# First four weight tiles sliced by chunk and multiplied beside the input's chunks, on one Trainium2 core

## The chip, the core and the metric

The kernel runs on one core of a Trainium2 chip. The metric is the device time of one execution in microseconds. Three runs of the kernel before gave 1047.52, 1047.68 and 1048.74 us, median 1047.68. Engines are named as the profile names them: PE is TensorE's matmul, PEld its weight load, DVE is VectorE, ACT is ScalarE, POOL is GpSimd, SP is SyncE, which issues the DMAs.

## The reference, cut to what matters

The reference is two transformer blocks of width 1024 on 512 tokens, in float32. What the change touches is the very beginning of the first block, the norm and the first part of its input projection:

```
h = x * rsqrt(mean(x * x) + 1e-6) * norm_mix_pre
proj = h @ w_in                      # 1024 -> 5120 columns
conv_in, q, k, v, g_conv, g_att = split(proj)
u = conv_in[:, :512] * sigmoid(conv_in[:, 512:])     # GLU, 8 tiles of 128 columns
u = causal depthwise convolution of 31 taps over u   # and so on
```

Attention, convolution branch, merge, feed-forward and the second block follow and stay as they are.

## The kernel before, in words

Activations lie transposed: 128 partitions are 128 features, 512 columns are the tokens, and the 1024 features are 8 chunks (KC). The weights come from HBM as a stream of 160 units. One unit is what one output tile of 128 features needs from all 8 chunks, 128x1024 floats, 512 KB. It lands in one of four slots of w_raw.

To keep float32 accuracy with the fast matmul, each operand is split in two parts: a high part (a_hi, w_hi), rounded by ACT with a Copy, and a low part (a_lo, w_lo), the rest, which DVE makes for the activations and POOL for most weights by a subtraction of two SBUF operands. A product of one chunk is three matmuls into the same bank: hi by hi (L442), activations' low by weights' high (L443), weights' low (L444). So a unit is 24 matmuls of 128x512.

The norm is applied late. The matmuls use x times the gain alone; the factor of each token, 1/rms, is multiplied in when DVE drains a bank (`drain`, L1624) with scale_row. For scale_row ACT squares the 8 chunks (sq_x, L1082), DVE adds them in place in seven steps (`add_square`, L1601), PE sums over partitions (`total`, L476, which waits for acc_ready and takes bank 6), DVE and ACT make the root (`norm`, `std`), PE turns it into a row (`spread`, L509, bank 7), and ACT copies the row (`row`, L1061). No tile can be drained before that.

Each engine works through an order written out by hand, with semaphores between engines. The beginning, before the change:

- SP (L404 to L414) issues the gain, then the eight chunks of x (256 KB each) with the two halves of unit 0 among them, then units 1, 2 and 3, then the other vectors. After that `load` (L416) refills a slot of w_raw when lo_ready says that its last unit has been split.
- ACT (L1067 to L1087) makes a_hi of each chunk as it lands, w_hi of unit 0's halves after chunks 0 and 2, then unit 1's, then the squares with unit 2's w_hi after two of them, then units 3, 4 and 5 as slots come free.
- DVE (L1613 to L1621) makes a_lo of each chunk (`low_scaled`, L1565), three half low parts of units 0 and 1 (`half_low`), then the seven adds, then the norm.
- POOL makes constants (L2191 to L2217), then the last half of unit 1's low part (L2225), then units' low parts in order (`ahead`, `low_weights`, L2185), of units 2 to 5 in the first round of its loop.
- PE (L529 to L556) waits for all 14 constants, then computes unit 0 chunk by chunk as chunks come, then units 1 and 2, `total`, unit 3 with `spread` in its middle, then units 4 to 7, of which 4 and 5 reuse banks 0 and 1 and wait for their drain, then the token tiles of v (L516).

After its norm DVE drains tiles 0 to 3, with a GLU product after each pair, and then works on the convolution's taps (`some_taps`, L1631, which accumulates in banks 4 and 5) with the drains of later tiles between them (L1742 to L1763).

Of the kernel before, what the change touches and what calls it, by code (L numbers as in the profile page):

```python
# [7 lines left out]
F32 = mybir.dt.float32  # L8
# [6 lines left out]
P = 128  # L15
# [63 lines left out]
def two_layer_block(nc, xT, vecs, wstream, outT):  # L79
    with ExitStack() as ctx:  # L80
# [12 lines left out]
        def sem(name):  # L93
            return ctx.enter_context(nc.semaphore(name))
# [160 lines left out]
        half_loaded, half_hi, half_lo = sem("half_loaded"), sem("half_hi"), sem("half_lo")  # L255
# [143 lines left out]
        @block.sync  # L399
        def _(sp_eng):  # L400
            def load_x(c):
                sp_eng.dma_start(resid[:, c, :], xT[:, c, :]).then_inc(x_loaded[c], 16)

            sp_eng.dma_start(vec[:, 0:KC], vecs[:, 0:KC]).then_inc(gain_loaded, 16)  # L404
            load_x(0)
            sp_eng.dma_start(w_raw[:, 0, 0:UNIT // 2], wstream[0][:, 0:UNIT // 2]).then_inc(half_loaded, 16)
            load_x(1)
            load_x(2)
            sp_eng.dma_start(w_raw[:, 0, UNIT // 2:], wstream[0][:, UNIT // 2:]).then_inc(raw_loaded[0], 16)
# [25 lines left out]
            sp_eng.wait_ge(stored, 16 * KC)  # L435
# [3 lines left out]
        def _(pe):  # L439
# [76 lines left out]
            def token_tiles(u0):  # L516

                for u in range(4):
# [7 lines left out]
                                          w_hi[:, u % 2, w], w_lo[:, u % 2, w], first=c == 0, last=c == KC - 1)  # L526
                    mm.then_inc(units_done, 1)

            pe.wait_ge(consts, CONSTS)  # L529


            for c in range(KC):
                pe.wait_ge(split_lo, c + 1)
                if c % 4 == 0:
                    pe.wait_ge(half_lo, c // 4 + 1)
                w = slice(c * P, (c + 1) * P)
                mm = products(ps[:, 0, :], w_hi[:, 0, w], w_lo[:, 0, w], a_hi[:, c, :], a_lo[:, c, :],
                              first=c == 0, last=c == KC - 1)
            mm.then_inc(units_done, 1)
            for c in range(KC):  # L540
                if c == 0:
                    pe.wait_ge(half_lo, 3)
                if c == KC // 2:
                    pe.wait_ge(lo_ready, 2)
                w = slice(c * P, (c + 1) * P)
                mm = products(ps[:, 1, :], w_hi[:, 1, w], w_lo[:, 1, w], a_hi[:, c, :], a_lo[:, c, :],
                              first=c == 0, last=c == KC - 1)
            mm.then_inc(units_done, 1)
            unit_tile(2, 0, 2, a_hi, a_lo)
            total(sq_x, 1)  # L550
            unit_tile(3, 1, 3, a_hi, a_lo, middle=lambda: spread(r_exp0, 0))
            for n in range(4, 8):
                pe.wait_ge(tile_drained, CREDIT + (n - 3 if n < 6 else 1))
# [478 lines left out]
        def _(act):  # L1032
# [34 lines left out]
            for c in range(KC):  # L1067
                act.wait_ge(x_loaded[c], 16)
                act.activation(a_hi[:, c, :], resid[:, c, :], ACT.Copy, scale=col("g_mix_pre", c)).then_inc(split_hi, 1)
                if c == 0:  # L1070
                    act.wait_ge(half_loaded, 16)
                    act.activation(w_hi[:, 0, 0:UNIT // 2], w_raw[:, 0, 0:UNIT // 2], ACT.Copy).then_inc(half_hi, 1)
                if c == 2:
                    act.wait_ge(raw_loaded[0], 16)
                    act.activation(w_hi[:, 0, UNIT // 2:], w_raw[:, 0, UNIT // 2:], ACT.Copy).then_inc(half_hi, 1)
            act.wait_ge(raw_loaded[1], 16)
            act.activation(w_hi[:, 1, 0:UNIT // 2], w_raw[:, 1, 0:UNIT // 2], ACT.Copy).then_inc(half_hi, 1)
            act.activation(w_hi[:, 1, UNIT // 2:], w_raw[:, 1, UNIT // 2:], ACT.Copy).then_inc(hi_ready, 1)
            for c in range(KC):
                if c == 2:  # L1080
# [468 lines left out]
        def _(dve):  # L1549
# [57 lines left out]
            def half_low(n):  # L1607
                k, at_half = n // 2, n % 2
                w = slice(at_half * UNIT // 2, (at_half + 1) * UNIT // 2)
                dve.wait_ge(half_hi, n + 1)  # L1610
                low(w_lo[:, k, w], w_raw[:, k, w], w_hi[:, k, w]).then_inc(half_lo, 1)
# [134 lines left out]
            for n, (a, b) in ((4, (0, 6)), (5, (6, 12)), (None, (12, 14)), (6, (14, 19)), (7, (19, 25)), (None, (25, 27))):  # L1746
# [435 lines left out]
        def _(pool):  # L2182
# [26 lines left out]
            for h in range(8):  # L2209
# [241 lines left out]
def _stream(w_in, w_conv_branch, w_att_branch, w_out, w_up, w_down, w_in_2, w_out_2):  # L2451
# [67 lines left out]
```

## Time and profile before

| | us |
|---|---|
| median of three runs | 1047.68 |
| the profiled execution's own time | 1047.43 |
| its span, first to last instruction | 1045.7 |
| PE busy in the span | 1025.2 |
| DVE busy | 522.4 |
| ACT busy | 458.4 |
| POOL busy | 519.2 |

The span is what the profiler saw between the first and the last instruction of the program; 1.7 us of the execution's own time lie outside it. A row of the timeline has the start in us from the span's begin, the time taken, the engine, the line, the operation with output and inputs, the shapes, a count of instructions merged into the row, and in brackets how long the engine sat idle before it and what ended that. The durations of matmuls overlap, because they are pipelined; from one start to the next is what a matmul costs.

### The profile page before, as it was taken

The numbers are of one execution on the slowest core, as the hardware profiler recorded it, in microseconds if no ns is written. First come the engines' busy times: TensorE is split into PE (matmuls) and PEld (weight loads), VectorE is DVE, ScalarE is ACT, GpSimd is POOL, SyncE is SP. The second block draws the span as 40 slices with busy tenths as digits, with TensorE's granted clock in tenths as the row PEclk, the third lists the DMA queues.
The fourth block names the chain that finished last, engine by engine and source line by source line (L and its number), as shares of the span: only waits on it lengthen the run. The fifth ranks groups of instructions, "written<-read, shape, count | busy, mean of one in ns | idle before, by whom it ended". The sixth has DMA issues, their size and how long they took to land.

```text
span 1045.7 us, 13313 instructions
## 1 busy us (share of the span) xinstructions
PE 1025.2 (98%) x4898; PEld 844.2 (81%) x4898; DVE 522.4 (50%) x839; ACT 458.4 (44%) x667; POOL 519.2 (50%) x300
## 2 busy tenths in 40 slices
PE   7999999999999999999999999999999999999998
PEld 5888888788888787888888888887888777777787
DVE  6899785554362555434434311003624176685731
ACT  5322345888752433223332222223354357476540
POOL 3444565933534423444444446445286554665562
PEclk9999999999999999999999999999999999999999
DMA  6233221111142313222232233324122211111112
GB/s 236 94 101 100 83 85 57 61 61 61 61 181 83 118 41 101 94 87 100 100 100 94 88 112 108 101 100 141 41 80 81 81 61 42 61 60 42 41 61 81
DMA packets 25965, 91.03 MB, mean 87 GB/s; under 512 B 3008, under 2 KB 3136, under 8 KB 25792
## 3 DMA queue, kind: packets, MB, share of 16 engines
q1 hardware_dynamic: 25920, 90.42, 25.7%
q8 instruction: 30, 0.49, 0.2%
q14 instruction: 15, 0.12, 0.0%
HBM read 88.31 MB, written 2.10 MB: 86 GB/s over the span
## 4 chain that ended last, share of the span: by engine, by line
PE 86%; DVE 5%; POOL 3%; issue 3%; ACT 2%; DMA 0%; SPq 0%; POOLq 0%; DVEq 0%; ACTq 0%
PE ps L442 26%; PE ps L444 26%; PE ps L443 26%; POOL w_lo L2185 2%; DVE s L2026 1%; PE ps L839 1%; PE ps L863 1%; PE ps L588 1%; POOL sp_lo L2237 1%; PE ps L582 1%; PE ps L484 1%; PE ps L568 1%; PE ps L471 0%; ACT s L1409 0%; DVE pt_lo L1562 0%
## 5 line engine op out<-in xcount | busy, mean ns | idle before, releaser
L2185 POOL TENSOR_TENSOR w_lo<-w_raw,w_hi 128x1024 fp32r<-128x1024 f32 x146 | 347.6, 2381 | 422.5 <-ACT w_hi L1040 373.1
L1040 ACT ACTIVATE w_hi<-w_raw 128x1024 fp32r<-128x1024 f32 (+1 forms) x140 | 146.3, 1045 | 287.4 <-PE ps L444 287.3
L442 PE MATMUL ps<-a_hi,w_hi 128*128 128x512 f32 x560 | 224.3, 400 | 9.9 <-DVE w_lo L1562 7.2
L444 PE MATMUL ps<-a_hi,w_lo 128*128 128x512 f32 x560 | 219.1, 391 | 0.0
L443 PE MATMUL ps<-a_lo,w_hi 128*128 128x512 f32 x560 | 219.0, 391 | 0.0
L442 PE MATMUL ps<-b_hi,w_hi 128*128 128x512 f32 x408 | 159.4, 391 | 1.0 <-POOL w_lo L2185 0.8
L444 PE MATMUL ps<-b_hi,w_lo 128*128 128x512 f32 x408 | 158.8, 389 | 0.0
L443 PE MATMUL ps<-b_lo,w_hi 128*128 128x512 f32 x408 | 158.7, 389 | 0.0
L442 PEld LDWEIGHTS ps<-a_hi,w_hi 128*128 128x128 f32 x560 | 105.6, 189 | 36.1 <-issue 9.1
L444 PEld LDWEIGHTS ps<-a_hi,w_lo 128*128 128x128 f32 x560 | 105.6, 189 | 22.8
L443 PEld LDWEIGHTS ps<-a_lo,w_hi 128*128 128x128 f32 x560 | 105.9, 189 | 21.1 <-issue 0.5
L442 PEld LDWEIGHTS ps<-b_hi,w_hi 128*128 128x128 f32 x408 | 76.6, 188 | 17.4 <-POOL w_lo L2185 1.2
L444 PEld LDWEIGHTS ps<-b_hi,w_lo 128*128 128x128 f32 x408 | 76.6, 188 | 16.0
L443 PEld LDWEIGHTS ps<-b_lo,w_hi 128*128 128x128 f32 x408 | 76.6, 188 | 15.8
L1645 DVE SCALAR_TENSOR_TENSOR ps<-u_pad,vec,ps 128x512 f32<-128x512 f32 x112 | 75.5, 748 | 0.0
L443 PE MATMUL ps<-h_lo,w_hi 128*128 128x512 f32 x176 | 68.5, 389 | 0.0
L444 PE MATMUL ps<-h_hi,w_lo 128*128 128x512 f32 x176 | 68.5, 389 | 0.0
L442 PE MATMUL ps<-h_hi,w_hi 128*128 128x512 f32 x176 | 68.5, 389 | 0.0
L1558 DVE TENSOR_TENSOR up_h<-up_u,up_s 128x512 f32<-128x512 f32 x22 | 49.4, 2246 | 21.5 <-ACT up_s L1302 21.3
L1558 DVE TENSOR_TENSOR up_u<-ps,scale_row 128x512 f32<-128x512 f32 x22 | 15.2, 690 | 83.4 <-PE ps L444 83.4
L1558 DVE TENSOR_TENSOR sq_f<-sq_f 128x512 f32<-128x512 f32 x13 | 9.8, 752 | 82.5 <-ACT sq_f L1326 81.9
L1409 ACT ACTIVATE s<-s,smax 128x384 f32<-128x384 f32 (+2 forms) x64 | 35.2, 552 | 16.8 <-DVE smax L2009 16.8
(324 smaller groups left out, 1591.8 us busy)
## 6 DMA issues: line engine op xcount, KB each, us to landing
w_raw<-weights SPq DMA_DIRECT2D x159, 512.0 KB, 3.2
resid<-x_t SPq DMA_DIRECT2D x8, 256.0 KB, 5.3
resid<-x_t SPq DMA_DIRECT2D x1, 2048.0 KB, 8.0
out_t<-out_sb SPq DMA_DIRECT2D x8, 256.0 KB, 2.0
w_raw<-weights SPq DMA_DIRECT2D x2, 256.0 KB, 4.5
vec<-vecs SPq DMA_DIRECT2D x1, 220.0 KB, 8.3
vec<-vecs SPq DMA_DIRECT2D x1, 4.0 KB, 1.8
```

The costliest lines, as they stand in the source:

```text
L442: pe.matmul(out, s_hi, m_hi, start=first, stop=False, skip_group_check=True)
L443: pe.matmul(out, s_hi, m_lo, start=False, stop=False, skip_group_check=True)
L444: return pe.matmul(out, s_lo, m_hi, start=False, stop=last, skip_group_check=True)
L484: pe.matmul(ps[:, 5, :], tri[:, :], src, start=True, stop=True, skip_group_check=True)
L568: pe.matmul(z_of(h)[:, o:o + (TB - j) * P], k[r, key], q[r, j * P:T], start=j != 3 and t == 0, stop=False, skip_group_check=True)
L582: pe.matmul(z[:, w], tri[:, :], parts[:, w], start=False, stop=False, skip_group_check=True)
L588: mm = pe.matmul(z[:, o:o + width], neg_ones[:, :], parts[:, Z_COL[j2]:Z_COL[j2] + width], start=False, stop=False, skip_group_check=True)
L1040: act.activation(w_hi[:, k % 2, 0:width], w_raw[:, k, 0:width], ACT.Copy).then_inc(hi_ready, 1)
L1409: e = act.activation(s2[:, head, w], s2[:, head, w], ACT.Exp, scale=-1.0, bias=smax[:, head, b:b + 1], accum_out=den[:, kind_of(c), half_o ...
L1558: return dve.tensor_tensor(out, in0, in1, op)
L1645: V.do(dve.scalar_tensor_tensor(out=acc if k == TAPS - 1 else part, in0=src, scalar=w, in1=part, op0=ALU.mult, op1=ALU.add))
L2185: pool.tensor_tensor(w_lo[:, k % 2, 0:width], w_raw[:, k, 0:width], w_hi[:, k % 2, 0:width].bitcast(F32), ALU.subtract).then_inc(lo_ready, 1)
```

## The change

The first four units are no longer stored tile by tile but chunk by chunk. The host packs units 0 to 3 so that one slice, 128x512, holds the weights of one chunk for all four tiles. Slices are loaded alternately with the chunks of x. PE multiplies chunk by chunk into four banks. Their high and low parts lie in buffers of their own (wf_hi, wf_lo, in the place of b_hi and b_lo), so units 4 and 5 find both slots of w_hi and w_lo free. POOL makes six of the eight low slices, DVE the first two. The sum of the squares (`total`) stands before the last chunk's matmuls, `spread` after them. Tile 4 gets bank 4 and no wait, and DVE drains it before the taps begin. ACT makes the high parts of units 4 and 5 right after the squares. Sixteen matmuls on a constant (WARM) stand ahead of everything on PE.

```
+WARM = 16
+        wf_hi = place("wf_hi", [P, KC, UNIT // 2], F32R, at["b_hi"])
+        wf_lo = place("wf_lo", [P, KC, UNIT // 2], F32R, at["b_lo"])
+        def slices(c):
+            return w_raw[:, c // 2, c % 2 * (UNIT // 2):(c % 2 + 1) * (UNIT // 2)]
-        GLU_BANKS, QK_BANKS, LO_BANKS = (0, 1, 2, 3, 0, 1, 6, 7), (6, 7), (0, 6, 7, 6)
+        GLU_BANKS, QK_BANKS, LO_BANKS = (0, 1, 2, 3, 4, 1, 6, 7), (6, 7), (0, 6, 7, 6)
 # SP
-            load_x(0)
-            sp_eng.dma_start(w_raw[:, 0, 0:UNIT // 2], ...).then_inc(half_loaded, 16)
-            load_x(1)
-            load_x(2)
-            sp_eng.dma_start(w_raw[:, 0, UNIT // 2:], ...).then_inc(raw_loaded[0], 16)
-            for c in range(3, KC):
+            for c in range(KC):
                 load_x(c)
-            for k in range(1, 4):
-                sp_eng.dma_start(w_raw[:, k, :], wstream[k]).then_inc(raw_loaded[k], 16)
+                load_slices(c)
             sp_eng.dma_start(vec[:, KC:], vecs[:, KC:]).then_inc(vec_loaded, 16)
...
-            sp_eng.wait_ge(half_lo, 3)
 # PE
+            pe.wait_ge(consts, 6)
+            for _ in range(WARM):
+                pe.matmul(ps[:, 5, 0:P], neg_ones[:, :], neg_ones[:, :], start=True, stop=True, ...)
             pe.wait_ge(consts, CONSTS)
             for c in range(KC):
+                if c == KC - 1:
+                    total(sq_x, 1)
+                pe.wait_ge(split_hi, c + 1)
+                pe.wait_ge(slice_hi, c + 1)
+                for k in range(4):
+                    pe.matmul(ps[:, k, :], wf_hi[:, c, k * P:(k + 1) * P], a_hi[:, c, :], ...)
                 pe.wait_ge(split_lo, c + 1)
+                for k in range(4):
+                    pe.matmul(ps[:, k, :], wf_hi[:, c, k * P:(k + 1) * P], a_lo[:, c, :], ...)
+                if c < 2:
+                    pe.wait_ge(slice_lo_v, c + 1)
+                else:
+                    pe.wait_ge(slice_lo_p, c - 1)
+                for k in range(4):
+                    mm = pe.matmul(ps[:, k, :], wf_lo[:, c, k * P:(k + 1) * P], a_hi[:, c, :], ...)
+                    if c == KC - 1:
+                        mm.then_inc(units_done, 1)
+            spread(r_exp0, 0)
+            unit_tile(4, 0, GLU_BANKS[4], a_hi, a_lo)
+            for n in range(5, 8):
+                pe.wait_ge(tile_drained, CREDIT + (2 if n == 5 else 1))
                 unit_tile(n, n % 2, GLU_BANKS[n], a_hi, a_lo)
 # ACT
             for c in range(KC):
                 act.wait_ge(x_loaded[c], 16)
                 act.activation(a_hi[:, c, :], resid[:, c, :], ACT.Copy, ...).then_inc(split_hi, 1)
+                act.wait_ge(raw_loaded[c // 2] if c % 2 else even_loaded[c // 2], 16)
+                act.activation(wf_hi[:, c, :], slices(c), ACT.Copy).then_inc(slice_hi, 1)
+            act.wait_ge(slice_hi, KC)
+            act.sem_inc(hi_ready, 4)
             for c in range(KC):
-                if c == 2:
-                    ahead(0, 0)
                 act.activation(sq_x[:, c, :], resid[:, c, :], ACT.Square).then_inc(sq_ready, 1)
-            ahead(0, 1)
+            for k in (0, 1):
+                act.wait_ge(raw_loaded[k], 2 * 16)
+                act.activation(w_hi[:, k, :], w_raw[:, k, :], ACT.Copy).then_inc(hi_ready, 1)
             std(0)
 # DVE
             for c in range(KC):
                 dve.wait_ge(split_hi, c + 1)
                 low_scaled(a_lo[:, c, :], resid[:, c, :], ...).then_inc(split_lo, 1)
-                if c in (0, 2):
-                    half_low(c // 2)
-            half_low(2)
+                if c < 2:
+                    dve.wait_ge(slice_hi, c + 1)
+                    low(wf_lo[:, c, :], slices(c), wf_hi[:, c, :]).then_inc(slice_lo_v, 1)
             for c in range(1, KC):
                 add_square(sq_x, 0, c)
...
+                if p:
+                    V.wait()
+                    glu_drain(4)
                 glu_product(p)
-            for n, (a, b) in ((4, (0, 6)), (5, (6, 12)), (None, (12, 14)), ...):
+            for n, (a, b) in ((5, (0, 12)), (None, (12, 14)), ...):
 # POOL
-            pool.wait_ge(hi_ready, 2)
-            pool.tensor_tensor(w_lo[:, 1, UNIT // 2:], ...).then_inc(lo_ready, 1)
-            with pool.Fori(0, 4) as i:
+            pool.wait_ge(slice_lo_v, 2)
+            pool.sem_inc(lo_ready, 1)
+            for c in range(2, KC):
+                pool.wait_ge(slice_hi, c + 1)
+                pool.tensor_tensor(wf_lo[:, c, :], slices(c), wf_hi[:, c, :].bitcast(F32), ALU.subtract).then_inc(slice_lo_p, 1)
+                if c % 2:
+                    pool.wait_ge(slice_lo_p, c - 1)
+                    pool.sem_inc(lo_ready, 1)
+            for k in (0, 1):
+                low_weights(1, k)
+            with pool.Fori(1, 4) as i:
 # host
+    first = np.stack(glu[:4]).reshape(4, P, 4, 2, P).transpose(2, 1, 3, 0, 4).reshape(4, P, UNIT)
+    glu = [*first, *glu[4:]]
```

## Rows read from the trace of the kernel before

**Rows 1.** The page's first part: busy us, share, instructions of each engine.

```profile
PE 1025.2 (98%) x4898; PEld 844.2 (81%) x4898; DVE 522.4 (50%) x839; ACT 458.4 (44%) x667; POOL 519.2 (50%) x300
```

**Rows 2.** Waits of PE, whole span: who waited for whom, us, times, longest.

```profile
PE ps L442 <- DVE w_lo L1562: 7.2, 1, 7.2
PE ps L863 <- DVE s L2026: 3.0, 3, 1.6
```

**Rows 3.** Timeline of PE, 7 to 33 us.

```profile
7.15 0.77 PE L442 MATMUL ps<-a_hi,w_hi 128*128 128x512 f32 x1 [7.15 <-DVE w_lo L1562]
...
10.84 0.63 PE L444 MATMUL ps<-a_hi,w_lo 128*128 128x512 f32 x1
11.27 0.63 PE L442 MATMUL ps<-a_hi,w_hi 128*128 128x512 f32 x1
...
12.23 0.40 PE L442 MATMUL ps<-a_hi,w_hi 128*128 128x512 f32 x1
...
25.87 0.95 PE L471 MATMUL ps<-ones,sq_x 128*128 128x1 f32 x8
...
29.55 0.60 PE L513 MATMUL ps<-ident,r_exp 128*128 128x128 f32 x4
29.90 0.48 PE L442 MATMUL ps<-a_hi,w_hi 128*128 128x512 f32 x1
...
32.75 0.39 PE L442 MATMUL ps<-a_hi,w_hi 128*128 128x512 f32 x1
```

**Rows 4.** Timeline of ACT, 5 to 20 us.

```profile
5.65 0.63 ACT L1072 ACTIVATE w_hi<-w_raw 128x512 fp32r<-128x512 f32 x1 [0.54 <-DMA w_raw<-weights]
...
11.84 0.72 ACT L1069 ACTIVATE a_hi<-resid,vec 128x512 fp32r<-128x512 f32 x1 [0.32 <-DMA resid<-x_t]
...
13.22 0.63 ACT L1077 ACTIVATE w_hi<-w_raw 128x512 fp32r<-128x512 f32 x1 [0.66 <-DMA w_raw<-weights]
...
16.27 3.22 ACT L1082 ACTIVATE sq_x<-resid 128x512 f32<-128x512 f32 x6
```

**Rows 5.** Timeline of POOL, 1 to 19 us.

```profile
1.52 0.20 POOL L2196 MEMSET neg_ones<- 128x128 f32 x1
...
14.46 1.31 POOL L2225 TENSOR_TENSOR w_lo<-w_raw,w_hi 128x512 fp32r<-128x512 f32 x1 [10.34 <-ACT w_hi L1078]
...
16.45 2.41 POOL L2185 TENSOR_TENSOR w_lo<-w_raw,w_hi 128x1024 fp32r<-128x1024 f32 x1 [0.68 <-ACT w_hi L1040]
```

**Rows 6.** Timeline of DVE, 12 to 21 us.

```profile
12.60 0.75 DVE L1565 SCALAR_TENSOR_TENSOR a_lo<-resid,vec,a_hi 128x512 fp32r<-128x512 f32 x1 [0.20 <-ACT a_hi L1069]
...
16.92 2.48 DVE L1558 TENSOR_TENSOR sq_x<-sq_x 128x512 f32<-128x512 f32 x1 [0.61 <-ACT sq_x L1082]
...
19.51 0.69 DVE L1558 TENSOR_TENSOR sq_x<-sq_x 128x512 f32<-128x512 f32 x1
...
20.30 0.69 DVE L1558 TENSOR_TENSOR sq_x<-sq_x 128x512 f32<-128x512 f32 x1
```

**Rows 7.** Timelines of POOL and DVE at 207 us and at 971 us.

```profile
207.02 2.41 POOL L2185 TENSOR_TENSOR w_lo<-w_raw,w_hi 128x1024 fp32r<-128x1024 f32 x1 [0.34 <-ACT w_hi L1040]
...
208.06 1.91 DVE L1720 SCALAR_TENSOR_TENSOR conv_acc<-conv_acc,vec,q_raw 128x512 f32<-128x512 f32 x1
...
971.48 1.89 DVE L2026 SCALAR_TENSOR_TENSOR s<-s,fac 128x512 f32<-128x512 f32 x1
...
971.51 1.31 POOL L2338 TENSOR_TENSOR k_lo<-y_qk,k_hi 128x512 fp32r<-128x512 f32 x1
972.75 2.86 POOL L2185 TENSOR_TENSOR w_lo<-w_raw,w_hi 128x1024 fp32r<-128x1024 f32 x1
```

**Rows 8.** Timeline of DVE, 37 to 93 us.

```profile
37.14 0.81 DVE L1555 TENSOR_SCALAR ps<-u_pad,vec 128x512 f32<-128x512 f32 x1
...
83.39 0.68 DVE L1558 TENSOR_TENSOR q_raw<-ps,scale_row 128x512 f32<-128x512 f32 x1
...
92.79 0.69 DVE L1558 TENSOR_TENSOR q_raw<-ps,scale_row 128x512 f32<-128x512 f32 x1 [0.64 <-PE ps L444]
```

More of the change, by code:

```diff
@@ L254, in two_layer_block @@
         x_loaded = [sem(f"x_loaded{n}") for n in range(KC)]
-        half_loaded, half_hi, half_lo = sem("half_loaded"), sem("half_hi"), sem("half_lo")
+        even_loaded = [sem(f"even_loaded{n}") for n in range(4)]
+        slice_hi, slice_lo_v, slice_lo_p = sem("slice_hi"), sem("slice_lo_v"), sem("slice_lo_p")
         raw_loaded = [sem(f"raw_loaded{n}") for n in range(4)]
@@ L402, in load_x, with load_slices @@
                 sp_eng.dma_start(resid[:, c, :], xT[:, c, :]).then_inc(x_loaded[c], 16)
+            def load_slices(c):
+                w = slice(c % 2 * (UNIT // 2), (c % 2 + 1) * (UNIT // 2))
+                sp_eng.dma_start(w_raw[:, c // 2, w], wstream[c // 2][:, w]
+                                 ).then_inc(raw_loaded[c // 2] if c % 2 else even_loaded[c // 2], 16)
             sp_eng.dma_start(vec[:, 0:KC], vecs[:, 0:KC]).then_inc(gain_loaded, 16)
-            load_x(0)
-            sp_eng.dma_start(w_raw[:, 0, 0:UNIT // 2], wstream[0][:, 0:UNIT // 2]).then_inc(half_loaded, 16)
-            load_x(1)
-            load_x(2)
-            sp_eng.dma_start(w_raw[:, 0, UNIT // 2:], wstream[0][:, UNIT // 2:]).then_inc(raw_loaded[0], 16)
-            for c in range(3, KC):
+            for c in range(KC):
                 load_x(c)
-            for k in range(1, 4):
-                sp_eng.dma_start(w_raw[:, k, :], wstream[k]).then_inc(raw_loaded[k], 16)
+                load_slices(c)
             sp_eng.dma_start(vec[:, KC:], vecs[:, KC:]).then_inc(vec_loaded, 16)
@@ L527, in token_tiles @@
                     mm.then_inc(units_done, 1)
+            pe.wait_ge(consts, 6)
+            for _ in range(WARM):
+                pe.matmul(ps[:, 5, 0:P], neg_ones[:, :], neg_ones[:, :], start=True, stop=True, skip_group_check=True)
             pe.wait_ge(consts, CONSTS)
             for c in range(KC):
-                pe.wait_ge(split_lo, c + 1)
[L534 to L553, printed above, removed]
+                if c == KC - 1:
[3 more added lines that the diff above has]
+                for k in range(4):
+                    pe.matmul(ps[:, k, :], wf_hi[:, c, k * P:(k + 1) * P], a_hi[:, c, :], start=c == 0, stop=False, skip_group_check=True)
@@ new lines, in _ @@
+                pe.wait_ge(split_lo, c + 1)
+                for k in range(4):
+                    pe.matmul(ps[:, k, :], wf_hi[:, c, k * P:(k + 1) * P], a_lo[:, c, :], start=False, stop=False, skip_group_check=True)
+                if c < 2:
[3 more added lines that the diff above has]
+                for k in range(4):
+                    mm = pe.matmul(ps[:, k, :], wf_lo[:, c, k * P:(k + 1) * P], a_hi[:, c, :], start=False, stop=c == KC - 1,
+                                   skip_group_check=True)
+                    if c == KC - 1:
+                        mm.then_inc(units_done, 1)
@@ L1069, in _ @@
                 act.activation(a_hi[:, c, :], resid[:, c, :], ACT.Copy, scale=col("g_mix_pre", c)).then_inc(split_hi, 1)
-                if c == 0:
-                    act.wait_ge(half_loaded, 16)
-                    act.activation(w_hi[:, 0, 0:UNIT // 2], w_raw[:, 0, 0:UNIT // 2], ACT.Copy).then_inc(half_hi, 1)
-                if c == 2:
[L1074 to L1078, printed above, removed]
+                act.wait_ge(raw_loaded[c // 2] if c % 2 else even_loaded[c // 2], 16)
+                act.activation(wf_hi[:, c, :], slices(c), ACT.Copy).then_inc(slice_hi, 1)
+            act.wait_ge(slice_hi, KC)
+            act.sem_inc(hi_ready, 4)
             for c in range(KC):
-                if c == 2:
-                    ahead(0, 0)
                 act.activation(sq_x[:, c, :], resid[:, c, :], ACT.Square).then_inc(sq_ready, 1)
-            ahead(0, 1)
+            for k in (0, 1):
+                act.wait_ge(raw_loaded[k], 2 * 16)
+                act.activation(w_hi[:, k, :], w_raw[:, k, :], ACT.Copy).then_inc(hi_ready, 1)
             std(0)
             act.preload_act_table(ACT.Sigmoid)
-            ahead(0, 2)
             row(0, scale_row)
@@ L1094, in _ @@
             glu(0, 0)
-            ahead(0, 3)
             glu(0, 1)
@@ L1605, in add_square @@
                 add(tt(sq[:, 0, :], sq[:, 0, :], sq[:, c, :], ALU.add))
[L1607 to L1611, printed above, removed]
             for c in range(KC):
@@ L1744, in _ @@
                 glu_drain(2 * p + 1)
+                if p:
+                    V.wait()
+                    glu_drain(4)
                 glu_product(p)
-            for n, (a, b) in ((4, (0, 6)), (5, (6, 12)), (None, (12, 14)), (6, (14, 19)), (7, (19, 25)), (None, (25, 27))):
+            for n, (a, b) in ((5, (0, 12)), (None, (12, 14)), (6, (14, 19)), (7, (19, 25)), (None, (25, 27))):
                 some_taps(a, b)
@@ L2218, in _ @@
             pool.wait_ge(consts, 14)
-            pool.wait_ge(half_hi, 2)
-            pool.sem_inc(hi_ready, 1)
-            pool.wait_ge(half_lo, 2)
+            pool.wait_ge(slice_lo_v, 2)
             pool.sem_inc(lo_ready, 1)
-            pool.wait_ge(hi_ready, 2)
-            pool.tensor_tensor(w_lo[:, 1, UNIT // 2:], w_raw[:, 1, UNIT // 2:], w_hi[:, 1, UNIT // 2:].bitcast(F32),
-                               ALU.subtract).then_inc(lo_ready, 1)
-            with pool.Fori(0, 4) as i:
+            for c in range(2, KC):
[7 more added lines that the diff above has]
+            with pool.Fori(1, 4) as i:
                 for k in range(4):
```

## The prediction

> **What bounds the kernel now.** I read the page first: PE is busy 98% of the span [rows 1], so only PE's idle time and slow matmuls can be given back. The waits of PE say where it idles: 7.2 us once, ahead of its first matmul, and after that never over 1.6 us at a time [rows 2]. Then the timeline of the first 33 us, engine by engine. PE's first matmul starts at 7.15; up to 11.27 starts lie 0.43 us apart, and a matmul takes 0.63; from 12.23 it takes 0.40 [rows 3], and twelve of them stand between 29.90 and 32.75, 0.23 apart with their lead-in. That is TensorE's clock at its lower level (1.2 GHz) until about 11.8 and at 2.4 GHz after. So the beginning loses 7.15 us of waiting and some 11 matmuls at 0.20 us each, 2.2 us. Everything later hangs on PE, so what PE has won or lost when it starts unit 4 (32.75 us, [rows 3]) comes out at the end. The question is when that point comes in the changed kernel.
>
> **Start.** The first slice is where unit 0's first half was in the queue, so its high part starts at 5.65 and takes 0.63 [rows 4]: PE starts at 6.3 instead of 7.15, since the low part is needed only by the ninth matmul. The sixteen matmuls on neg_ones can begin when it is set, 1.52 + 0.20 [rows 5]. No row shows them at the low clock. Four 128-column transposes at the high clock hold PE from 29.55 to 29.90, 0.09 each [rows 3]; doubled, 16 x 0.18 = 2.9 us, ending at 4.6. The upper bound is a full 0.43 each, 6.9 us, ending at 8.6. The lower bound is nothing, they end before 6.3. I take the lower, the shape being that of the transposes.
>
> **PE's work in the eight chunks.** Twelve matmuls a chunk at 0.227 (24 to a unit of 5.44 us) are 2.72 us. With the clock up from the start PE has done seven chunks at 6.3 + 19.1 = 25.4. If the warm-up does nothing and the clock rises at 11.8 as before, 13 matmuls cost 0.20 more: 28.0. If the warm-up runs to 8.6 but lifts the clock: 27.7. Data is no limit: with the x chunk landed tenth at 11.84 and unit 1, 512 KB, at 13.22 [rows 4], 256 KB take 0.69, so x and slice of a chunk take 1.4 us against 2.7 on PE, and the last slice lands near 16.0.
>
> **What PE then meets: the sum of squares.** Its `total` stands before the eighth chunk and waits for DVE's seventh add. Before, the adds were ready when PE came (25.87, no wait). Now ACT does a_hi and a slice for all eight chunks first; the last slice is done at 16.6, the squares start at 16.7 instead of 14.28 and come 0.52 apart (six in 3.22, [rows 4]); after them unit 4's high part, 20.9 to 21.9, and unit 5's to 23.0. POOL subtracts six slices and then units 4 and 5. And POOL and DVE exclude each other when both read two SBUF operands:
>
> - An add starts at 16.92 under POOL's 16.45 to 18.86 and takes 2.48, ending 0.54 after POOL [rows 5, 6]; alone adds follow at 0.80 [rows 6].
> - The same holds for a scalar_tensor_tensor of two SBUF tensors, which is what a_lo is: 1.91 instead of 0.75, ending 0.54 after POOL's 209.43 [rows 7].
> - With both queued they alternate: DVE 971.48 to 973.37 under POOL's 971.51 to 972.82; then POOL's next, issued at 972.75, takes 2.86, that is it ends at 975.61, 2.25 after DVE's end, where one alone takes 2.41 [rows 5, 7]. A 512-column one that waited costs accordingly 1.31 - 0.15 = 1.16.
>
> So from chunk 2 on a_lo and POOL's slice go in turns, 0.54 + 1.16 = 1.70 us a chunk, though ACT delivers every 1.4. DVE has finished a_lo of chunk 2 at 9.8; six slices and the five a_lo between them, 6 x 1.16 + 5 x 0.54 = 9.66, end at 19.5. The first add, queued since about 18, ends at 20.0. The second and third at 0.80 follow, the fourth starts at 21.7, against POOL's unit 4 at about 22.0. Then turns again: POOL to 24.7, fifth add 25.2, POOL's unit 5 to 27.45, sixth add 28.0, seventh 28.8. If POOL is first instead, the fourth and fifth are held, the last ends at 29.1. Bounds: only one of POOL's two units falls among the adds, 26.5; turns cost 0.1 more each, 29.8. I take 28.8, the row of 971 us being exactly this pattern.
>
> **Sum.** PE comes between 25.4 and 28.0 and goes on at 28.85, whatever the clock did. `total` and twelve matmuls then take 29.55 - 25.87 = 3.68 and `spread` 0.35 [rows 3]. The factors are there in time: before, `spread` came 3.68 after `total` too. Unit 4 starts at 32.88 against 32.75: +0.13, with POOL first +0.4; I take +0.2. Against the profiled execution's own 1047.43 that is 1047.6; the median shown is 0.25 above that execution, so 1047.9.
>
> **The rest, at nothing.** SP issues eighteen transfers instead of fifteen before its loop, the same bytes; the ones in flight hide the three more issues. Unit 4's load goes out after the first two low slices and is needed at 20.9. Unit 4's low part is ready at 24.7, unit 5's at 27.45, both wanted after 32.9. Tile 4 has a free bank, so its wait is gone; it was covered anyway, as PE did not stand there. DVE's taps start later: the first drain comes 1.26 after `spread`, tile 4 ends at 38.3 and is drained, product, taps from 40.0 against 37.14 [rows 8], 2.9 late, of which 0.6 is the drain done ahead. Behind these taps the tile of q drained at 83.39 to 84.07 goes to 86.4; PE wants its bank when the tile drained at 92.79 starts, 92.79 - 5.44 = 87.35. That cover is 1.0 us; were it gone, PE would be late by what DVE is over. At 92.79 DVE waits for PE again and the lateness is over [rows 8].
>
> **Rules weighed.** The rows show the exclusion for adds and for a multiply-subtract, none for a_lo itself, which had no POOL work beside it. The Trainium skill, "SBUF — State Buffer", section "SBUF: two separate sides", says that a VectorE instruction with two SBUF inputs and a GpSimd one that reads SBUF hold a shared port pair exclusively, whichever starts first; by that rule a_lo is blocked, and the sum stands; without it the first rival's time comes out. The Trainium skill, "TensorE: Matmul & The Clock Gate", section "What's actually happening", says that activity releases the throttle and idleness brings it back; the first half speaks for the warm-up, which the sum doesn't need, the second for the clock rival below.
>
> **Rivals.**
>
> 1. a_lo is not held, 12%. For it: the rows show the hold for another line only. Then slices end at 17.9, the adds run from 18.5, five more by 22.5, the seventh is held by unit 4 and done at 25.3. PE doesn't wait: unit 4 starts at 25.4 + 4.03 = 29.4, 3.3 us early: 1044.4. With two adds held instead of one 27.6: 1046.7.
> 2. Only one unit of POOL's falls among the adds, 10%. It needs unit 5's high part later than 27, or the adds 3 us earlier; ACT has nothing before it. 26.5: 2.2 early, 1045.5.
> 3. Slower: TensorE's clock falls while PE waits for the adds. The wait is 3.4 us if the warm-up worked, longer than any since the clock rose (1.6, [rows 2]), so no row says that it stays up. Price as in the beginning, 11 matmuls at 0.20: 2.2 more, 1050.1. It decides once PE comes early enough, near 25.4, and only then; 12%.
> 4. The taps' lateness exceeds the cover at 87 us, by 1 to 2 us, 5%: 1049.4.
> 5. The warm-up fails to lift the clock: no change to the time, as PE comes at 28.0, still before 28.85. It is inside the forecast.
>
> **How the numbers follow.** The forecast has 61%, its own range being 1047.3 to 1049.0. A measurement of this kernel can tell 0.2%, 2.1 us, from no change. Faster than 1045.6: most of rival 1 and half of 2, 0.16. Slower than 1049.8: rival 3 and a little of 4, 0.14. Same: 0.70. The range that leaves out 2 in 10 goes from 1045.0 to 1050.2.
>
> **What would show it.** PE's first real matmul at 6.3; a_lo of chunks 3 to 7 at 1.2 us or more each with POOL's slices in between; PE idle 1 to 3.5 us before the eight one-column matmuls, ended by DVE's sq_x add near 28.8; two adds of some 2.8 us each; unit 4 starting near 32.9. The prediction is wrong if PE doesn't wait there, if a_lo takes 0.75 beside POOL, or if matmuls take 0.63 us again after that wait.

## The result, and the profile after

The changed kernel takes 1049.84 us (median of 22 executions, 1047.61 to 1051.35); the kernel before, on the same chip, 1047.60 (22, 1047.13 to 1048.74). The ratio is 1.0017 [1.0011, 1.0024]: slower, by less than the 0.2% that count as a difference here, though the interval reaches a little past it. Of the runs further below, one execution of run 1 (1138.19 us, mean granted clock 0.852) is in a slow state and is left out.

Behind the median stand two kinds of executions. Seven lie at 1047.61 to 1048.53, with TensorE's mean granted clock at 1.000; fifteen lie at 1049.68 to 1051.35, with 0.998 or 0.997. The second kind is called the dearer one below. All executions of the kernel before are at 1.000 or 0.999. These means count the time up to the clock's first record, 11.7 us in the profile below, as full speed; what the clock was there is read from the durations of the matmuls.

The profiled execution took 1048.31 us (span 1046.4) and is of the first kind; before's took 1047.43 (span 1045.7). Busy time of the engines, beside [rows 1]:

```profile
PE 1029.5 (98%) x4914; PEld 848.2 (81%) x4914; DVE 525.7 (50%) x838; ACT 458.9 (44%) x669; POOL 523.0 (50%) x303
```

PE has 16 matmuls more, the warm-up, and with their 3.68 us is busy 4.3 us longer. The wait of 7.15 us ahead of the first matmul is gone, and a new one stands at `total` (L478); the waits behind the start are those of the kernel before. Waits of PE, whole span:

```profile
PE ps L873 <- DVE s L2026: 3.0, 3, 1.6
PE ps L538 <- POOL neg_ones L2196: 1.8, 1, 1.8
...
PE ps L478 <- DVE sq_x L1561: 1.3, 1, 1.3
```

Timeline of PE, in place of [rows 3]:

```profile
1.77 3.68 PE L538 MATMUL ps<-neg_ones 128*128 128x128 f32 x16 [1.77 <-POOL neg_ones L2196]
5.89 2.04 PE L547 MATMUL ps<-a_hi,wf_hi 128*128 128x512 f32 x4 [0.44 <-ACT wf_hi L1081]
7.73 1.91 PE L550 MATMUL ps<-a_lo,wf_hi 128*128 128x512 f32 x4
...
13.26 1.07 PE L556 MATMUL ps<-a_hi,wf_lo 128*128 128x512 f32 x4
...
29.23 1.05 PE L478 MATMUL ps<-ones,sq_x 128*128 128x1 f32 x8 [1.30 <-DVE sq_x L1561]
...
32.98 0.60 PE L520 MATMUL ps<-ident,r_exp 128*128 128x128 f32 x4
33.33 0.48 PE L449 MATMUL ps<-a_hi,w_hi 128*128 128x512 f32 x1
```

The timeline says three things. The first real matmul starts 1.26 us earlier than before (5.89 against 7.15), but a group of four takes 1.91 us, that is starts 0.43 apart, so the warm-up has not lifted TensorE's clock; from 13.26 a group takes 1.07, and the level changes at 11.7 (11.8 before). PE then stands for 1.30 us until 29.23. And unit 4 begins at 33.33 against 32.75: +0.58. After that PE's gaps are one for one those of before, and the last matmul is 0.68 late.

What PE waits for is DVE, which is held by POOL. Timelines of DVE and POOL, 13 to 30 us, in place of [rows 5, 6]:

```profile
13.47 1.78 DVE L1568 SCALAR_TENSOR_TENSOR a_lo<-resid,vec,a_hi 128x512 fp32r<-128x512 f32 x1
...
15.17 1.78 DVE L1568 SCALAR_TENSOR_TENSOR a_lo<-resid,vec,a_hi 128x512 fp32r<-128x512 f32 x1
...
16.88 1.78 DVE L1568 SCALAR_TENSOR_TENSOR a_lo<-resid,vec,a_hi 128x512 fp32r<-128x512 f32 x1
18.58 1.79 DVE L1561 TENSOR_TENSOR sq_x<-sq_x 128x512 f32<-128x512 f32 x1
20.48 0.69 DVE L1561 TENSOR_TENSOR sq_x<-sq_x 128x512 f32<-128x512 f32 x1
...
22.07 2.71 DVE L1561 TENSOR_TENSOR sq_x<-sq_x 128x512 f32<-128x512 f32 x1
24.88 2.70 DVE L1561 TENSOR_TENSOR sq_x<-sq_x 128x512 f32<-128x512 f32 x1
...
28.48 0.69 DVE L1561 TENSOR_TENSOR sq_x<-sq_x 128x512 f32<-128x512 f32 x1
```

```profile
14.66 1.75 POOL L2224 TENSOR_TENSOR wf_lo<-w_raw,wf_hi 128x512 fp32r<-128x512 f32 x1
...
18.07 1.75 POOL L2224 TENSOR_TENSOR wf_lo<-w_raw,wf_hi 128x512 fp32r<-128x512 f32 x1
...
21.82 2.41 POOL L2185 TENSOR_TENSOR w_lo<-w_raw,w_hi 128x1024 fp32r<-128x1024 f32 x1 [2.00 <-ACT w_hi L1088]
```

An a_lo (the three shown are of chunks 5 to 7) takes 1.78 us in place of 0.75 [rows 6], and they lie 1.70 and 1.71 apart. The fourth and fifth add take 2.7 us each, behind POOL's two units; the seventh ends at 29.17, PE goes on at 29.23.

The taps start at 40.50 against 37.14 [rows 8], and PE doesn't feel it. Timeline of DVE:

```profile
40.50 0.81 DVE L1558 TENSOR_SCALAR ps<-u_pad,vec 128x512 f32<-128x512 f32 x1
```

### The profile page after: what moved, and what is told of

Read it like the earlier page. It is cut to its first block, busy times and chain, and to the rows that moved or that the text cites. A ratio compares the mean times of both kernels' runs of the same rounds, so it can differ in the third digit from the quotient of the medians.

```text
span 1046.4 us, 13351 instructions
## 1 busy us (share of the span) xinstructions
PE 1029.5 (98%) x4914; PEld 848.2 (81%) x4914; DVE 525.7 (50%) x838; ACT 458.9 (44%) x669; POOL 523.0 (50%) x303
## 4 chain that ended last, share of the span: by engine, by line
PE 84%; DVE 6%; POOL 3%; issue 3%; ACT 2%; DMA 1%; SPq 0%; DVEq 0%; POOLq 0%; ACTq 0%
PE ps L449 25%; PE ps L450 25%; PE ps L451 25%; POOL w_lo L2185 2%; DVE s L2026 1%; PE ps L849 1%; PE ps L873 1%; PE ps L598 1%; DVE sq_x L1561 1%; POOL sp_lo L2240 1%; PE ps L592 1%; PE ps L491 1%; PE ps L578 1%; DMA resid<-x_t 1%; DVE a_lo L1568 1%
## 5 line engine op out<-in xcount | busy, mean ns | idle before, releaser
L2185 POOL TENSOR_TENSOR w_lo<-w_raw,w_hi 128x1024 fp32r<-128x1024 f32 x144 | 343.2, 2384 | 423.4 <-ACT w_hi L1050 372.0
L1050 ACT ACTIVATE w_hi<-w_raw 128x1024 fp32r<-128x1024 f32 x136 | 142.1, 1045 | 277.1 <-PE ps L451 277.1
L449 PE MATMUL ps<-a_hi,w_hi 128*128 128x512 f32 x528 | 210.4, 399 | 2.8 <-DVE v_lo L1565 1.6
L451 PE MATMUL ps<-a_hi,w_lo 128*128 128x512 f32 x528 | 205.9, 390 | 0.0
L450 PE MATMUL ps<-a_lo,w_hi 128*128 128x512 f32 x528 | 205.6, 389 | 0.0
L449 PEld LDWEIGHTS ps<-a_hi,w_hi 128*128 128x128 f32 x528 | 99.1, 188 | 27.2 <-DVE v_lo L1565 2.9
L451 PEld LDWEIGHTS ps<-a_hi,w_lo 128*128 128x128 f32 x528 | 99.1, 188 | 21.4
L450 PEld LDWEIGHTS ps<-a_lo,w_hi 128*128 128x128 f32 x528 | 99.3, 188 | 19.7 <-issue 0.5
```

The source lines that it names most:

```text
L449: pe.matmul(out, s_hi, m_hi, start=first, stop=False, skip_group_check=True)
L450: pe.matmul(out, s_hi, m_lo, start=False, stop=False, skip_group_check=True)
L451: return pe.matmul(out, s_lo, m_hi, start=False, stop=last, skip_group_check=True)
L1050: act.activation(w_hi[:, k % 2, 0:width], w_raw[:, k, 0:width], ACT.Copy).then_inc(hi_ready, 1)
L2185: pool.tensor_tensor(w_lo[:, k % 2, 0:width], w_raw[:, k, 0:width], w_hi[:, k % 2, 0:width].bitcast(F32), ALU.subtract).then_inc(lo_ready, 1)
```

## The experiments

The theory at their start: PE's wait for the adds explains the 0.6 us of the cheaper executions; in the others TensorE's clock falls on account of that wait, and this makes the median. The rival: in those executions the adds themselves end later.

**1. same.** The changed kernel once more, for a trace of the dearer kind.

> The changed kernel unchanged, for a second trace. Theory: DVE's seventh add ends near 29.2 us in every execution, and PE's wait for it is short (1.3 us) where PE ran at the low clock until 11.7, and long (some 4 us) where the warm-up lifted the clock early; in the latter the clock falls again during the wait and costs up to 2 us more. So executions of two kinds, near 1048.4 and near 1049.9 us, and a trace of the second kind shows matmuls of 0.39 us before 25 us, a wait near 4 us, and matmuls of 0.63 us after it. Rival: the clock has nothing to do with it, the adds end later in the second kind (30.7 us), and matmuls after the wait take 0.39.

1049.21 us, ratio 1.0013 [1.0004, 1.0021] (11 executions). Five of the 11 have the lower mean clock, and the profiled one is of them: 1051.94, span 1050.0. Its timeline of PE:

```profile
29.62 1.40 PE L478 MATMUL ps<-ones,sq_x 128*128 128x1 f32 x8 [2.31 <-DVE sq_x L1561]
30.87 2.05 PE L547 MATMUL ps<-a_hi,wf_hi 128*128 128x512 f32 x4
32.73 1.91 PE L550 MATMUL ps<-a_lo,wf_hi 128*128 128x512 f32 x4
34.43 1.91 PE L556 MATMUL ps<-a_hi,wf_lo 128*128 128x512 f32 x4
36.14 1.02 PE L520 MATMUL ps<-ident,r_exp 128*128 128x128 f32 x4
36.84 0.54 PE L449 MATMUL ps<-a_hi,w_hi 128*128 128x512 f32 x1
```

PE goes on only 0.39 later than in the other profile (29.62 against 29.23), so the rival has 0.39 of the 3.63 us between the two executions. Nearly all the rest is the clock: groups of four take 1.91 again. Busy time and granted clock (the column before the last two) by stretches of 2 us say the same:

```profile
28.00:30.00 2.00, 0.38 (x4) 0.39 (x4) 1.39 (x2) 0.00 (x0) 0.00 (x0) 1.00 0.64 188
30.00:32.00 2.00, 2.00 (x9) 1.81 (x10) 0.64 (x4) 0.73 (x2) 0.00 (x0) 0.54 0.18 74
32.00:34.00 2.00, 2.00 (x6) 1.52 (x5) 0.97 (x4) 0.73 (x1) 0.00 (x0) 0.50 0.00 0
...
36.00:38.00 2.00, 2.00 (x10) 1.70 (x9) 0.17 (x1) 0.60 (x1) 0.00 (x0) 0.75 0.00 0
```

0.50 is the level of 1.2 GHz; it lasts from 30.16 to 36.99, so it begins 0.54 after the wait has ended and not in it. Price: twelve products at 0.20 more, 2.4; `total` takes 1.25 until the next product starts, against 0.91, and `spread` 0.70 against 0.35: 3.1 us in all. In this execution the clock had risen at 9.7 instead of 11.7, so PE came sooner and waited longer, 2.31 us against 1.30; I had expected near 4. That the other executions of the dearer kind lose their time at the same place is not traced.

**2. nowarm.** The sixteen matmuls on neg_ones left out.

```diff
-WARM = 16
+WARM = 0
```

> WARM = 0, the sixteen matmuls on a constant are gone. Theory (PE goes on when the adds are done, the warm-up only lengthens the wait and lets the clock fall in it): PE reaches the wait at 26.5 to 28, goes on at 29.2, no execution of the slower kind, all near 1048.4 us, 1.4 under the changed kernel's median. Rival (warm-up is worth what it gives the first chunks, 2 us): 1050 or more, above the changed kernel.

1048.74 us (11 executions), ratio 1.0016 [1.0007, 1.0025]. Seven are at 1048.26 to 1048.82, four at 1050.06 to 1052.43. My expectation that the dearer kind would go was wrong: it comes without the warm-up too. Whether the warm-up makes it more frequent, 4 of 11 against 5 of 11 and 15 of 22, these counts don't settle. Timeline of PE in the profiled execution (1048.26):

```profile
29.20 1.05 PE L478 MATMUL ps<-ones,sq_x 128*128 128x1 f32 x8 [0.62 <-DVE sq_x L1561]
```

The clock rises at 12.4, PE waits 0.62 us, and the clock stays up. PE's early start is worth nothing here: products begin at 6.56 instead of 5.89, and PE goes on at 29.20 as it did at 29.23.

**3. late_low.** POOL begins units 4 and 5 only after the adds.

```diff
+            pool.wait_ge(acc_ready, 1)
             for k in (0, 1):
                 low_weights(1, k)
```

> The changed kernel with POOL's low parts of units 4 and 5 held until the seventh add is done (one more wait for acc_ready on POOL). Theory (port shared by POOL and DVE delays the adds): adds 4 and 5 fall from 2.7 to 0.69 us, the seventh ends at 25.2 instead of 29.2, PE waits under 0.5 us; unit 4 starts near 29.3 if the clock was up from the start and near 32 if it rose at 11.7. Time 1044.5 to 1046.5 us, 1 to 3 below the kernel before. Rival (the adds are bound by something else, ACT's squares or the late start of DVE): adds unchanged, 1048.4 to 1049.9.

1046.94 us (1045.61 to 1048.16, 11 executions), ratio 0.9990 [0.9981, 0.9998], no execution of the dearer kind. Its interval lies clear of that of run 1. Timelines of DVE and of PE:

```profile
18.52 6.56 DVE L1561 TENSOR_TENSOR sq_x<-sq_x 128x512 f32<-128x512 f32 x7
```

```profile
27.15 1.07 PE L556 MATMUL ps<-a_hi,wf_lo 128*128 128x512 f32 x4
28.06 0.95 PE L478 MATMUL ps<-ones,sq_x 128*128 128x1 f32 x8
...
32.09 0.48 PE L449 MATMUL ps<-a_hi,w_hi 128*128 128x512 f32 x1
```

Seven adds end at 25.1 instead of 29.2, `total` has no wait, and unit 4 starts 0.66 before [rows 3] and 1.24 before the changed kernel. So the two held adds are the wait. The median is 0.4 above the 1044.5 to 1046.5 that I expected; in the profiled execution the clock rose late (12.1), so that PE came to `total` only at 28.06.

**4. before_warm.** The kernel before with the same sixteen matmuls ahead.

```diff
+            pe.wait_ge(consts, 6)
+            for _ in range(16):
+                pe.matmul(ps[:, 5, 0:P], neg_ones[:, :], neg_ones[:, :], start=True, stop=True, ...)
```

> The kernel before with only the sixteen matmuls on a constant added ahead of PE's first wait. Theory: the clock is up early in some executions, PE's first matmul stays at 7.15, the 11 slow matmuls become fast in those; but unit 0 then waits for the chunks (a_hi comes every 0.65 to 1.0 us against 0.68 us for three matmuls), so 0 to 1.5 us less than before: 1046 to 1047.6. Rival (warm-up matmuls do not lift the clock at all): 1047.6, and the trace shows 0.63 us matmuls until 11 us.

1047.84 us (11), ratio 1.0001 [0.9993, 1.001]. Timeline of PE:

```profile
1.78 3.67 PE L531 MATMUL ps<-neg_ones 128*128 128x128 f32 x16 [1.78 <-POOL neg_ones L2198]
7.08 0.77 PE L442 MATMUL ps<-a_hi,w_hi 128*128 128x512 f32 x1 [1.62 <-DVE w_lo L1564]
...
11.90 0.63 PE L444 MATMUL ps<-a_hi,w_lo 128*128 128x512 f32 x1
```

Still 0.63 a matmul at 11.90; here the level changes at 12.75. So this warm-up has no effect on the time that shows, in either kernel. One of these 11 executions took 1049.70, and two of the 35 of the kernel before 1049.94 and 1049.96, all three with a mean granted clock of 1.000: the mark of the dearer kind is the clock, not the time alone, and what those three lost is open.

**5. warm512.** Eleven matmuls of 128x512 on a tile of their own in place of the sixteen. The theory now says: with the clock up at once PE comes early, waits over 3 us, and the clock falls every time.

```diff
-WARM = 16
+WARM = 11
...
-            pe.wait_ge(consts, 6)
+            pe.wait_ge(warm_set, 1)
...
-                pe.matmul(ps[:, 5, 0:P], neg_ones[:, :], neg_ones[:, :], ...)
+                pe.matmul(ps[:, 5, :], warm_up[:, 0:P], warm_up[:, :], ...)
 # POOL, first
+            pool.memset(warm_up[:, :].bitcast(F32), -1.0).then_inc(warm_set, 1)
```

> The changed kernel with a stronger warm-up: eleven 128x512 matmuls on a constant (its own memset first on POOL) instead of sixteen 128x128, so PE is busy from about 1.3 to 5.9 us. Theory (the place where PE goes on is set by the adds, 29.2 us, and a clock that is up early only lengthens the wait): matmuls take 0.39 us from before 7 us, PE waits near 4 us from 25.3 to 29.2, the clock falls in nearly every execution and costs 1.5 to 3.5 more: 1050 to 1052. Rival (the clock lost in the first chunks was what the changed kernel lacks): 1045 to 1047.

1050.11 us (1049.78 to 1051.7), ratio 1.0029 [1.0019, 1.0039], and all 9 executions have the lower mean clock. Timeline of PE in the profiled one (1049.78):

```profile
1.37 4.91 PE L539 MATMUL ps<-warm_up 128*128 128x512 f32 x11 [1.37 <-POOL warm_up L2192]
6.46 1.16 PE L548 MATMUL ps<-a_hi,wf_hi 128*128 128x512 f32 x4 [0.17 <-ACT wf_hi L1082]
7.46 1.07 PE L551 MATMUL ps<-a_lo,wf_hi 128*128 128x512 f32 x4
...
29.07 1.16 PE L479 MATMUL ps<-ones,sq_x 128*128 128x1 f32 x8 [3.32 <-DVE sq_x L1562]
30.09 2.06 PE L548 MATMUL ps<-a_hi,wf_hi 128*128 128x512 f32 x4
...
34.77 0.48 PE L450 MATMUL ps<-a_hi,w_hi 128*128 128x512 f32 x1
```

The first products already run at 1.07 a group. All that this wins goes into the wait, 3.32 us, and the low level from 29.89 to 33.30, which again begins after the wait, costs on top: 34.77 - 29.07 = 5.70 from `total` to unit 4, against 4.10 with the clock up, 1.6 us. So the better warm-up makes the changed kernel slower: its fastest execution took 1049.78, where 7 of 22 with the small warm-up lie at 1048.53 or below.

**6. late_warm512.** Both: the adds free (3) and the clock up (5).

> The same warm-up with POOL's low parts of units 4 and 5 held until the seventh add is done. Theory: adds done at 25.1, PE arrives at 25.3, no wait, unit 4 starts near 29.4: 1044.2 to 1044.8, 3 below the kernel before. Rival (the warm-up cannot lift the clock before the real work does): as without it, 1046.9.

1044.93 us (1044.46 to 1047.25, 9 executions), ratio 0.9973 [0.9963, 0.9983]: faster than both kernels, though the interval does not clear the 0.2% in full. Against the 0.9990 of run 3 the warm-up is worth some 0.17% where no wait stands behind it. The profiled execution is the outlier, 1047.25, and shows the weak point; its timeline of PE:

```profile
1.37 4.12 PE L539 MATMUL ps<-warm_up 128*128 128x512 f32 x11 [1.37 <-POOL warm_up L2192]
7.41 1.79 PE L548 MATMUL ps<-a_hi,wf_hi 128*128 128x512 f32 x4 [1.91 <-ACT wf_hi L1082]
9.00 1.91 PE L551 MATMUL ps<-a_lo,wf_hi 128*128 128x512 f32 x4
```

The first slice came late there (it landed at 6.61, against 5.66 in run 5), and PE stood for 1.91 us after the warm-up. The clock, up since 4.3, fell at 7.69, after PE had gone on, and was low until 11.11, so it had won little. This fall has no one-column matmuls ahead of it, and a mean clock of 0.998 here comes from another place than `total`.

**7. total_after.** `total` behind the last chunk instead of ahead of it, `spread` in the middle of unit 4.

```diff
-                if c == KC - 1:
-                    total(sq_x, 1)
...
-            spread(r_exp0, 0)
-            unit_tile(4, 0, GLU_BANKS[4], a_hi, a_lo)
+            total(sq_x, 1)
+            unit_tile(4, 0, GLU_BANKS[4], a_hi, a_lo, middle=lambda: spread(r_exp0, 0))
```

> The changed kernel with total behind the eighth chunk instead of before it, and spread in the middle of unit 4 (POOL untouched, the adds still end at 29.2). Theory (only the place of PE's wait matters, not the adds' end): the eighth chunk covers the wait, PE comes to total at 28 to 30.7, waits 1.2 us at most, no fall of the clock; unit 4 with spread ends at 36.5 to 37.2 instead of 38.8: 1046.0 to 1046.8. Rival (the late norm only moves the wait to the drains, tile 5 waits for bank 1): 1048.4.

1047.42 us (1046.41 to 1048.36, 11), ratio 0.9998 [0.9989, 1.0007]; no execution of the dearer kind. The wait is gone: PE comes to `total` at 29.24, and the adds end at 28.90, as late as before. But a next one shows, 0.57 us for POOL's w_lo:

```profile
42.30 0.47 PE L449 MATMUL ps<-a_hi,w_hi 128*128 128x512 f32 x1 [0.57 <-POOL w_lo L2183]
```

I had expected 1046.0 to 1046.8; the profiled execution lies there (1046.41), the median is 1.0 above that execution. In the profiled one the clock rose early, at 9.2; that the others had it later is likely but not shown, and what they lose stays open.

**8. dve_slices.** All eight low slices on DVE, so that none of POOL's work falls among the a_lo.

```diff
-                if c < 2:
-                    pe.wait_ge(slice_lo_v, c + 1)
-                else:
-                    pe.wait_ge(slice_lo_p, c - 1)
+                pe.wait_ge(slice_lo_v, c + 1)
 # DVE: low(wf_lo[:, c, :], ...) for every c
 # POOL
-                pool.wait_ge(slice_hi, c + 1)
-                pool.tensor_tensor(wf_lo[:, c, :], slices(c), ...).then_inc(slice_lo_p, 1)
                 if c % 2:
-                    pool.wait_ge(slice_lo_p, c - 1)
+                    pool.wait_ge(slice_lo_v, c + 1)
```

> The changed kernel with all eight low slices made by DVE, none by POOL. Theory (POOL's slices and a_lo exclude each other, 1.70 us a chunk): a_lo and slices then take 0.75 and 0.69, a chunk 1.3 us, the first add ends near 18.3 instead of 20.4; POOL's units 4 and 5 still fall among the adds, the seventh ends near 27.2 to 28 instead of 29.2; unit 4 starts up to 1.5 us earlier: 1046.5 to 1048. Rival (a_lo is slow for itself beside ACT or DMA): a_lo stays at 1.78, the adds end at 29.2 or later.

1046.69 us (10 executions), ratio 0.9988 [0.9979, 0.9998]. Timeline of DVE:

```profile
16.07 0.75 DVE L1565 SCALAR_TENSOR_TENSOR a_lo<-resid,vec,a_hi 128x512 fp32r<-128x512 f32 x1
16.74 0.68 DVE L1562 TENSOR_TENSOR wf_lo<-w_raw,wf_hi 128x512 fp32r<-128x512 f32 x1
17.88 7.49 DVE L1558 TENSOR_TENSOR sq_x<-sq_x 128x512 f32<-128x512 f32 x7 [0.46 <-ACT sq_x L1082]
```

The seventh of these adds by itself:

```profile
22.65 2.71 DVE L1558 TENSOR_TENSOR sq_x<-sq_x 128x512 f32<-128x512 f32 x1
```

a_lo is back at 0.75, and DVE starts a new chunk every 1.3 us (both instructions together 1.43, overlapping by a little) where the pair of engines took 1.70. The adds start at 17.9 and end at 25.4: only the last is held (2.71), better than the 27.2 to 28 that I had expected. PE doesn't wait for them.

**9. before_warm512.** The kernel before with thirteen of the larger warm-ups.

> The kernel before with thirteen 128x512 matmuls on a constant ahead of PE's first wait, so the clock is up when the real work starts at 7.1 us. Theory (in the kernel before, the sum of squares stands right behind PE: adds end at 25.6 us, total came at 25.9): unit 0 then follows the chunks, units 1 and 2 end near 24, and PE waits at total for the adds, so that almost nothing of the 2.2 us of slow matmuls comes back: 1047.2 to 1047.6. Rival (PE alone bounds the beginning, the norm doesn't): 1045.5 to 1046.

1047.61 us (11), ratio 0.9996 [0.9987, 1.0005]. In the profiled execution, the slowest of the 11 (1048.05), the clock is up at 6.75, products start at 7.84 and follow 0.23 apart, and yet nothing comes back. The time is what I expected, the place isn't: PE doesn't wait at `total`, it waits for chunks ahead of it:

```profile
7.84 0.47 PE L443 MATMUL ps<-a_hi,w_hi 128*128 128x512 f32 x1 [0.74 <-DVE w_lo L1565]
...
10.38 0.50 PE L443 MATMUL ps<-a_hi,w_hi 128*128 128x512 f32 x1 [0.22 <-DVE a_lo L1568]
```

From 8 to 16 us PE is busy 6.74 of 8. The adds end at 26.18 there and PE comes to `total` at 26.44, so without the waits for chunks it would have met the wait that I expected. A warm clock gave next to nothing in the old order and some 0.17% in the new one (run 6 against run 3). That the slices by chunk are what lets it be used fits this, but two things differ, as the new order also has 12 matmuls more ahead of `total`; which of them counts for how much was not run.

**10. dve_warm512.** 8 and 5 together: POOL not held, clock up.

> The changed kernel with all low slices on DVE and the stronger warm-up, POOL's units 4 and 5 not held. Theory: the adds end at 25.4 as in dve_slices, PE arrives at 25.3, so the wait is under 0.5 us and the clock stays: 1044.6 to 1045.2, the same as with POOL held, because both remove the same wait. Rival (holding POOL is what matters): 1046 or more.

1045.05 us (1044.73 to 1045.75, 7), ratio 0.9973 [0.9962, 0.9984]: level with 6, and no dearer execution. Timeline of PE in the profiled one (1045.32):

```profile
7.07 1.17 PE L548 MATMUL ps<-a_hi,wf_hi 128*128 128x512 f32 x4 [0.68 <-ACT wf_hi L1079]
...
26.23 0.94 PE L479 MATMUL ps<-ones,sq_x 128*128 128x1 f32 x8
...
30.26 0.48 PE L450 MATMUL ps<-a_hi,w_hi 128*128 128x512 f32 x1
```

`total` has no wait, and unit 4 starts 2.5 ahead of [rows 3].

## Why the prediction was right, and where it wasn't

The forecast was 1047.9 with a range of 1045.0 to 1050.2; measured 1049.84. The class (within 0.2%) and the range hold, the class with some luck, as 1.0017 has 1.0024 in its interval. But the case that had 61%, in which PE waits for the adds until 28.85 and nothing else happens, describes 7 of 22 executions (their median 1048.36, 0.5 above the number). The median is made by rival 3, which had 12% and a price of 1050.1. The prediction named three signs of being wrong, and the third, matmuls of 0.63 us again after the wait, is what run 1 shows: right in the range, it was wrong in the mechanism for two executions in three. That rival 3's 1050.1 comes so near the 1049.89 of the dearer kind is luck in part: its base was 0.5 too low and its price, 2.2, was 0.7 too high.

- **Start.** 6.3 predicted, 5.89 measured: the first slice landed at 5.09, where unit 0's first half had landed at 5.63. It varies: 5.67 in run 1, 6.61 in run 6.
- **Warm-up.** I left its effect open, as PE goes on at the end of the adds "whatever the clock did", and that was right for the cheaper executions. Its sixteen matmuls took 3.68 us, not 2.9, and ended at 5.45, still before the products. Rival 5 is true as far as the traces go: in all six profiles with it the clock is low when the products begin.
- **The exclusion of POOL and DVE.** 1.70 us a chunk predicted from [rows 7], 1.70 and 1.71 measured between chunks 5 to 7 (less, 1.25 and 1.50, between 3 and 5); slices to 19.5, measured 19.8; adds to 28.8, or 29.1 with POOL first, measured 29.17 with POOL first (21.82 before 22.07). Rival 1 (a_lo is not held) is refuted, by 1.78 us here and 0.75 where POOL is quiet (run 8). The rule of the Trainium skill, "SBUF — State Buffer", section "SBUF: two separate sides", is borne out for a_lo as well, by these two numbers.
- **Rival 2.** Here both of POOL's units fell among the adds; with DVE earlier by 0.7 at the first add (17.88 against 18.58) and that add not held, only one did (run 8). So the rival's condition was right in kind and not in size: 3 us weren't needed.
- **The sum.** +0.2 predicted at unit 4, +0.58 measured. The end of the wait was 0.38 later than I took.
- **The taps.** 40.0 predicted, 40.50 measured, covered as worked out.
- **The clock.** The failed step is rival 3's condition: "It decides once PE comes early enough, near 25.4, and only then". I had tied the fall to a wait of 3.4 us, since the waits up to 1.6 of [rows 2] left the clock up. It fell after 2.31 us (run 1), with PE arriving at 27.3. How early PE comes depends on when the clock rose: at 12.4 it waited 0.62, at 11.7 1.30, at 9.7 2.31, at 6.0 3.32; in the last two the clock fell. So a case that I gave 12% came in 15 of 22 executions, going by their mean clock and their time; two profiles, of runs 1 and 5, show it at `total` itself. The Trainium skill, "TensorE: Matmul & The Clock Gate", section "What's actually happening", has idleness bringing the throttle back; the traces agree in kind for the waits of 2.31 and 3.32, and for the 1.91 of run 6, each with the fall 0.3 to 0.8 us after PE had gone on. The price was worked out right in kind, slow products at 0.20 each: 2.2 predicted, 1.6 for the low stretch of 3.4 us (run 5) and 3.1 for that of 6.8 (run 1).

That the wait causes the fall is shown by taking it away in three ways (runs 3, 7, 8: none of 32 executions at 0.998 or below) and by lengthening it (run 5: 9 of 9). Two of the 32 are at 0.999; in the profiled one of them the clock is low only from 1043.4 on, behind PE's last matmul. The eight one-column matmuls of `total` aren't enough by themselves, as runs 3, 7 and 8 have them without a fall, and they aren't needed, as the fall of run 6 came without them. How long a wait must be isn't shown: the clock fell after one of 1.91 us (run 6) and stayed after one of 1.30 and, later in the kernel, of 1.6 [rows 2], with different work around them.

The gain that the change could have was there: 2.7 and 2.9 us by the medians (runs 6 and 10). It needs both a warm-up that works and adds that end before PE comes.

## What to carry to other kernels

When more parts of a startup run side by side, look at the sum that all engines meet in, and whether VectorE and GpSimd both read two SBUF operands ahead of it: each pair then goes in turns, and the sum is late by the turns. A wait of TensorE as long as those here (a fall followed waits of 1.91, 2.31 and 3.32 us) is to be priced at its length plus a fall of the clock, and so making TensorE earlier in front of such a wait can cost time. Remove the wait first, then warm the clock, with matmuls of the size of the real ones.

## What the runs showed of the hardware that I had not expected

- Sixteen 128x128 matmuls, 0.23 us apart from 1.8 to 5.4, did not lift TensorE's clock to 2.4 GHz ahead of the products in any profile: it rose at 11.7, 9.7, 12.1, 9.2, 12.4 and 12.75 in kernels with them, and at 12.4 (nowarm) and 11.8 (before) without. Whether they bring the rise forward in some executions isn't shown. Eleven of 128x512 did, by 4.3 to 6.2 us, and thirteen by 6.75.
- The low level, once back, stayed for 3.41 us (warm512, 29.89 to 33.30), 3.42 (late_warm512) or 6.83 (same), though PE stood nowhere in it.
- The rise itself varies between executions of one kernel: 11.7 in the changed kernel's profile of 1048.31 us and 9.7 in that of 1051.94, where the earlier rise led to the longer wait.
- VectorE and GpSimd take turns when both have such work queued. DVE's held instruction ends 0.54 or 0.55 us after POOL's, an a_lo as well as an add: 13.54 after 12.99, 20.37 after 19.82, 24.78 after 24.23 in the changed kernel's profile.
